# Splitting the output projection's first weights inside the samples' attention, and turning the result rows inside the last MLP

## The reference

```
def run_trunk(x, pos, nsa_cache, page_table, win_cache, ...):
    for l in range(DEPTH):
        h = rms_norm(x, attn_norm_g[l])
        (q, k_cmp, v_cmp, k_slc, v_slc, k_win, v_win, gate_pre, hq, hf, hi, hg) = split_proj(h @ w_in[l])
        ...
        past = nsa_cache[l, page_table]            # samples: 8 pages of 128 rows each
        wk = concatenate([win_cache[l][:, :, 0], k_win])
        ...
        o_nsa = nsa_attention(...)                 # compressed, selected and window branches, with gates
        o_hg, s_fin = hgrn2(...)
        x = x + concatenate([o_nsa, o_hg]) @ w_out[l]
        h2 = rms_norm(x, mlp_norm_g[l])
        x = x + square(relu(h2 @ w_up[l])) @ w_down[l]
    return x, ...
```

## Time and profile before

| | |
|---|---|
| time, median of 3 runs | 2057.99 us (2055.7 to 2062.35) |
| the profiled execution's own time | 2054.93 us |
| its span | 2053.1 us |
| PE busy | 1905.8 us (93%) |
| DVE, ACT, POOL busy | 55%, 40%, 34% |
| mean granted PE clock | 0.966 |

### The profile page before, as it was taken

How to read it: one execution, slowest core, us unless ns; L and a number is a source line. 1 busy time by engine, 2 the same in 40 slices (tenths; PEclk the granted TensorE clock), 3 DMA queues, 4 the chain that set the end, 5 groups by cost and what they waited for, 6 DMA issues and landing times. The chain is left out here.

```text
span 2053.1 us, 38910 instructions
## 1 busy us (share of the span) xinstructions
PE 1905.8 (93%) x15789; PEld 1785.9 (87%) x15789; DVE 1138.6 (55%) x1899; ACT 828.1 (40%) x1809; POOL 692.3 (34%) x470
## 2 busy tenths in 40 slices
PE   6999798988799999999999997989887999999998
PEld 6999555988599999999999984668875999999998
DVE  4589655454455555555528886555535454545454
ACT  4594355353534131313146923544435341313130
POOL 2325435240043333333323542443201333333331
PEclk8999888999999999999999997999999999999999
DMA  4220520432522222222222223222254222222221
GB/s 155 86 80 23 164 66 9 117 93 70 158 83 83 83 83 84 82 87 83 78 85 84 63 73 104 58 64 67 83 154 111 83 71 93 78 92 81 85 82 48
DMA packets 200638, 175.80 MB, mean 86 GB/s; under 512 B 11356, under 2 KB 198030, under 8 KB 200334
## 3 DMA queue, kind: packets, MB, share of 16 engines
q1 hardware_dynamic: 200354, 173.30, 27.7%
q10 hardware_dynamic: 108, 0.03, 0.0%
HBM read 162.67 MB, written 10.62 MB: 84 GB/s over the span
## 5 line engine op out<-in xcount | busy, mean ns | idle before, releaser
L427 POOL TENSOR_TENSOR WX<-RAW,WX 128x2048 fp32r<-128x2048 f32 (+2 forms) x48 | 222.4, 4634 | 523.0 <-ACT WX L423 523.0
L2391 DVE TENSOR_TENSOR sq<-sq 128x288 f32<-128x288 f32 x128 | 156.9, 1231 | 196.8 <-ACT sq L2360 196.8
L427 POOL TENSOR_TENSOR m_wl<-RAW,m_wh 128x2048 fp32r<-128x2048 f32 x36 | 166.5, 4624 | 285.1 <-ACT m_wh L423 285.1
L439 PE MATMUL bank<-UH,m_wl 128*128 128x288 f32 x640 | 188.7, 295 | 0.0
L438 PE MATMUL bank<-UL,m_wh 128*128 128x288 f32 x640 | 188.7, 295 | 0.0
L437 PE MATMUL bank<-UH,m_wh 128*128 128x288 f32 x640 | 188.6, 295 | 0.0
L439 PE MATMUL bank<-UH,WX 128*128 128x288 f32 x576 | 170.0, 295 | 0.0
L438 PE MATMUL bank<-UL,WX 128*128 128x288 f32 x576 | 169.8, 295 | 0.0
L437 PE MATMUL bank<-UH,WX 128*128 128x288 f32 x576 | 169.6, 295 | 0.0
L2410 DVE TENSOR_TENSOR OT<-bank,rstd 128x288 f32<-128x288 f32 x128 | 58.2, 455 | 183.2 <-PE bank L439 183.2
L2413 DVE TENSOR_TENSOR XT<-XT,OT 128x288 f32<-128x288 f32 x128 | 156.3, 1221 | 4.4
(11 more groups left out here) (386 smaller groups left out, 5829.3 us busy)
## 6 DMA issues: line engine op xcount, KB each, us to landing
RAW<-in_w_up SPq DMA_DIRECT2D x32, 1024.0 KB, 5.4
RAW<-in_w_down SPq DMA_DIRECT2D x32, 1024.0 KB, 5.2
RAW<-in_w_in SPq DMA_DIRECT2D x20, 1024.0 KB, 5.3
R<-in_cache_nsa_kv SPq DMA_DIRECT2D x128, 64.0 KB
HT<-in_cache_nsa_kv SPq DMA_DIRECT2D x128, 64.0 KB, 2.6
RAW<-in_w_in SPq DMA_DIRECT2D x6, 1056.0 KB, 5.4
R<-in_cache_nsa_kv SPq DMA_DIRECT2D x48, 128.0 KB, 2.8
out<-R SPq DMA_DIRECT2D x10, 512.0 KB, 5.0
```

The source lines that it names most:

```text
L427: eng.tensor_tensor(S.granule(S.wl, i, w)[:, chunks], S.granule(S.raw, i, w)[:, chunks], S.granule(S.wh, i, w)[:, chunks].bitcast(F32), AL ...
L439: ins = pe.matmul(out, wl[:, c, cols], ah[:, c, n], start=False, stop=(c == KC - 1))
L2391: dve.tensor_tensor(relu[n % 4], relu[n % 4], relu[n % 4], ALU.mult).then_inc(sem("relu_squared"), 1)
```

## The change

Three things are changed.

1. **The first granule's split goes into the samples' attention.** SP loads the first two granules right behind the last sample's past, without its own wait. ACT makes the high part in its program of pair 2, behind the copies of the probabilities, and POOL makes the whole rest then. The MLP block begins with the copies of `OT`. `WX` must be there during the attention, so the attention's own tiles are smaller.
2. **Seven places for the past are written out** in a table, each of three pieces of 1024 words, so that a place may lie in pieces of several tiles. Sample 4's load starts with the block; samples 5 and 6 wait for `s_valued` (the first product of values on PE), where before only 6 did; sample 7 waits for the first pair's values as before.
3. **The result is turned inside the last MLP.** In the last quarter of `w_down` PE turns the prompt's columns of feature chunk m-1 (4 turns) behind the units of chunk m, ACT copies them into `Y`, and SP stores `Y` in four parts (chunks 0 to 3, 4 and 5, 6, 7). Behind the last unit PE turns the samples' 8 chunks and the prompt's last one. The last block, and the clearing of semaphores ahead of it, are gone.

```diff
@@ samples' attention @@
-                    for b in range(4, NB):
-                        if b == RING - 1:
-                            sp.wait_ge(sem("s_valued"), 1)
-                        if b >= RING:
-                            sp.wait_ge(sem("b_valued"), (b - RING) // 2 + 1)
-                        load_past(sp, b)
-                    sp.wait_ge(sem("b_valued"), 2)
+                    load_past(sp, 4)
+                    sp.wait_ge(sem("s_valued"), 1)
+                    load_past(sp, 5)
+                    load_past(sp, 6)
+                    sp.wait_ge(sem("b_valued"), 1)
+                    load_past(sp, 7)
                     for g in range(2):
                         load_out_granule(...)
+                @block.gpsimd
+                def _(pool):
+                    pool.wait_ge(sem("out_hi"), 1)
+                    pool.tensor_tensor(w0_part(1), W0, w0_part(0).bitcast(F32), ALU.subtract)
...
                             act.activation(dst, src, ACT.Copy).then_inc(sem("pT_kept"), 1)
+                        if a == 2:
+                            act.wait_ge(sem("m_w_raw0"), 16 * 3)
+                            act.activation(w0_part(0), W0, ACT.Copy).then_inc(sem("out_hi"), 1)
@@ MLP, PE @@
-                    pe.wait_ge(sem("m_first_lo"), 1)
-                    first_products(pe, bank[2:6], S7, 0, GW, "mix_lo", lambda c: c + 1, "m_w_lo", (UH, UL))
+                    def turn_prompt(c):
+                        pe.wait_ge(sem("m_grown"), 16 * 3 + 2 * c + 2)
+                        if c >= 2:
+                            pe.wait_ge(sem("y_kept"), c - 1)
+                        for t in range(NT):
+                            ins = pe.transpose(bank[c % 2][:, t * P:(t + 1) * P], XT[:, c, t * P:(t + 1) * P], ident)
+                        ins.then_inc(sem("y_turned"), 1)
...
+                    first_products(pe, bank[2:6], S7, 0, GW, "mix_lo", lambda c: c + 1, (UH, UL))
...
+                        if last and kind == "down" and q == 3 and s == 1 and m >= 1:
+                            turn_prompt(m - 1)
+                    if last:
+                        pe.wait_ge(sem("m_added"), RANK[-5])
+                        for c in range(KC - 1):
+                            turn_samples(c)
+                        turn_prompt(KC - 1)
+                        turn_samples(KC - 1).then_inc(sem("ys_turned"), 1)
@@ MLP, ACT @@
-                    split_hi(act, S7, 0, GW, 0)
+                    def keep_prompt(c):
+                        act.wait_ge(sem("y_turned"), c + 1)
+                        act.activation(Y[:, :, c * P:(c + 1) * P], bank[c % 2]..., ACT.Copy).then_inc(sem("y_kept"), 1)
@@ MLP, DVE @@
-                    split_lo(dve, S7, 0, GW, slice(0, KC // 2), "first_lo")
...
+                    if last:
+                        dve.wait_ge(sem("ys_turned"), 1)
+                        for i in range(2):
+                            ins = dve.tensor_copy(YS[:, i * 512:(i + 1) * 512], bank[2 + (len(U7) + i) % 6][0:NS, :])
+                        ins.then_inc(sem("ys_kept"), 1)
@@ MLP, SP @@
+                    if last:
+                        for a, b in ((0, 4), (4, 6), (6, 7), (7, 8)):
+                            sp.wait_ge(sem("y_kept"), b)
+                            sp.dma_start(y_prompt[0, :, a * P:b * P]..., Y[:, :, a * P:b * P]).then_inc(sem("y_stored"), 16)
+                        sp.wait_ge(sem("ys_kept"), 1)
+                        sp.dma_start(y_sample..., YS).then_inc(sem("y_stored"), 16)
```

More of the change, by code:

```diff
@@ L444, in keep_warm, with first_products @@
             pe.matmul(out[:, 0:n], ident, cst[:, 0:n], start=True, stop=True)
-        def first_products(pe, banks, S, i, w, done, counts, second_half=None, operand=None):
+        def first_products(pe, banks, S, i, w, done, counts, operand=None):
             wh, wl = S.granule(S.wh, i, w), S.granule(S.wl, i, w)
@@ L2042, in layer @@
             cmp_scope.close()
+            open_wx()
             smp_scope = ExitStack()
[L2044 to L2048, removed]
+            R2 = smp_scope.enter_context(nc.sbuf_tensor(f"R2s_{l}", [P, SLOT + 14 * P], F32))
+            KTS = smp_scope.enter_context(nc.sbuf_tensor(f"KTS_{l}", [P, 3072], F32, side="right"))
+            slots += [((R2, 0), (R2, 1024), (R2, 2048)), ((R1, 0), (R1, 1024), (R1, 2048)),
+                      ((HT_, 3072), (R2, 3072 + 14 * P), (R1, R_HI))]
+            assert len(slots) == max(PLACE) + 1
             kTb = [KTS[:, i * 1536:(i + 1) * 1536] for i in range(2)]
@@ L2138, in values @@
                         pe.wait_ge(sem("pT_kept"), 4 * a + 4)
-                        for i, (js, past, new) in enumerate(((range(8), past_of, 12), (range(8, 12), window_of, 13))):
+                        for i, (js, new) in enumerate(((range(8), 12), (range(8, 12), 13))):
                             for j in (*js, new):
@@ L2301, in _ @@
                 def _(pool):
-                    for i in range(len(G7)):
-                        split_lo(pool, S7, i, GW, slice(0 if i else KC // 2, KC))
+                    for i in range(1, len(G7)):
+                        split_lo(pool, S7, i, GW)
                     if l + 1 < DEPTH:
@@ L2364, in _ @@
                                 relu_hi(act, n)
+                        if last and kind == "down" and q == 3 and s == 1 and m >= 1:
+                            keep_prompt(m - 1)
                         if u % 4 == 3 and i + 2 < len(G7):
                             split_hi(act, S7, i + 2, GW, u + 1)
+                    if last:
+                        keep_prompt(KC - 1)
                     if l + 1 < DEPTH:
@@ L2417, in layer @@
                 wx[-1][0].close()
[L2418 removed]
+            else:
+                clear_semaphores()
         for l in range(DEPTH):
             layer(l)
[L2424 to L2453 removed]
```

102 lines of the change are left out of this document (41 added, 61 removed).

## The result

| | before | changed |
|---|---|---|
| time, median | 2057.99 us (2055.7 to 2062.35) | 2045.16 us (2044.31 to 2050.49) |
| span of the profiled execution | 2053.1 us | 2042.6 us |
| PE busy | 1905.8 us | 1903.5 us |
| mean granted PE clock | 0.966 | 0.970 |

The ratio of the times is 0.9943 with a 95% interval of 0.9923 to 0.9962, that is 11.7 us less (7.8 to 15.8). The forecast was 2046.0, with 2042 to 2051.5 as its range. Time, range and sign were right; of the sum's three terms the one for the clock was not.

The account below looks back on a forecast made before the run. Only PE's idle stretches, at MLP starts and the end, could be won. Savings of 7.2, 1.5 (clock) and 3.3 took 12.0 from 2054.9, giving 2042.9; the median's 3.1 offset made 2046.0 us, range 2042 to 2051.5.

Parts of the forecast that it names:

- The attention's end: End of the samples' attention: ACT's added round makes it 0.9 us later per layer, bounds nothing to 1.9.
- The first product: Start of each layer's MLP: PE's first product starts 3.6 us earlier, 7.2 for both layers.
- The clock: PE's clock at both MLP starts: four chances in ten each to keep 2.4 GHz, one keeping it likeliest, 1.5 us gained.
- The rival that the clock holds at both starts: Both MLP starts: PE keeps 2.4 GHz after the shorter gap, 1.5 us less, 2044.5; chance 0.13.
- The end: Last MLP and program's end: turning the result between products gives 3.3 us less, bounds 0.9 to 4.5.
- The sum: Whole kernel: 7.2 + 1.5 + 3.3 = 12.0 us less, bounds 6.1 to 16.5.
- the 3.1 that I carried over: Whole kernel: the runs' median stood 3.1 us above the profiled execution, assumed to hold after the change.
- The hold of POOL over pair 3's step: Samples' attention: POOL's work may delay DVE's step on `HT`; about 2 us were left, so costed at nothing.
- the slower rival: Last quarter of the last MLP: PE stands at turns waiting for late additions, 16 us lost, 2062; chance 0.03.
- the one in which nothing moves: Samples' attention: weights land late, so the MLP start's wait only changes its place, 2058; chance 0.04.
- The 7: Samples' attention: the early-issued weights land some 7 us before ACT needs them at 552.2.

Follow-up runs that it names:

- Experiment 3: The changed kernel with ACT's round of the first granule ahead of pair 2's copies of the probabilities, not behind them; 2047.25 us, 0.9942 to the kernel before.
- experiment 5: The kernel before with the first granule's rest made wholly by DVE, POOL only clearing one column of a scratch tile; 2056.34 us in one run.
- experiment 4: The changed kernel with PE multiplying unread constants behind the attention's last turns and ahead of the MLP's first product; 2044.21 us, 0.9932 to the kernel before.
- experiment 1: The changed kernel without the result's turns in the last MLP, the last block and semaphore clearing kept as before; 2052.29 us, 0.9969 to the kernel before.
- experiment 6: The changed kernel with SP again waiting for pair 1's values before it loads the output projection's first granules; 2047.63 us in one run.
- experiment 8: The changed kernel itself run once more, with a second profile; 2049.61 us, 0.9943 to the kernel before.
- experiment 7: The changed kernel with ACT's round ahead of pair 2's copies, PE's products of constants, and samples' rows copied in two steps; 2041.21 us, 0.9908 to the kernel before.

## Why the prediction was right, and where it was not

**The attention's end, 0.9 a layer: right.** Measured 1.0 and 0.9. Experiment 3 takes all but 0.1 of it away by moving ACT's round alone.

**The first product, 3.6 earlier: right.** Measured 3.6 and 3.8. The gap went to the predicted length, 2.69, and `UL` still ends it. Part of the old gap was POOL's hold on the first `UL`: by experiment 5 the second half of the rest cost 1.0 more on POOL than it would have on DVE.

**The clock: the step that failed.** The prediction gave each layer four chances in ten to keep 2.4 GHz, and took 1.5 us from "exactly one of the two". All ten starts with this gap (two layers in the changed kernel and in experiments 1, 3, 6 and 8) fell to 1.2 GHz, nine of them for 3.4 us and one for 6.8. The term was 0. Its price was right: 1.5 a layer, by experiment 4. The rival that the clock holds at both starts came out only where PE was kept at work (experiments 4 and 7).

The chances had been read from gaps elsewhere in the program, one that held and one that fell, as if the length of a gap told the odds. Nearer rows than those of rows 8 would not have corrected it. PE's timeline of the kernel before has the same gap of 2.73 us at the same place of either layer, and its windows show that the clock held after the first and fell after the second:

```profile
231.56 1.17 PE L926 MATMUL bank<-R,HT 32*128 32x128 f32 x32 [2.73 <-DVE R L1112]
...
1240.58 1.33 PE L926 MATMUL bank<-R,HT 32*128 32x128 f32 x22 [2.73 <-DVE R L1112]
```

```profile
232.00:235.00 3.00, 3.00 (x43) 1.23 (x36) 2.37 (x10) 0.00 (x0) 2.77 (x5) 1.00 0.85 239
1241.00:1244.00 3.00, 3.00 (x36) 1.27 (x29) 1.77 (x8) 0.00 (x0) 2.77 (x6) 0.50 0.85 239
```

Over all ten profiles the clock fell at this gap of 2.73 in 17 cases of 20. A gap of 2.1 at 448.2 held in the changed kernel's first profile (1.00 from 449 to 451) and fell in experiment 8's (0.50), with the same program. So the length alone does not decide. Experiment 4 shows that work in the gap keeps the clock; what besides the gap brings it down, and whether a start with this gap could ever hold, stays open.

The Trainium skill, in "TensorE: Matmul & The Clock Gate", "What's actually happening", ties the fall to a whole idle window. By it a short gap would be safe. The runs speak against that: in the first layers of experiments 1 and 3 the fall came 1.2 and 1.1 us after full-speed products had resumed. Ahead of the gap, though, PE had only four short turns between idle stretches of 0.80 and 2.69 us, so the gap was not the only idleness near the fall.

**The end, 3.3: the mechanism right, the size low.** It is 4.0: 6.8 at the end less 2.8 in the stretch with the six groups, of which they are 2.6. They were costed at 3.0. From the last scaling to the end I had 7.0, and it was 6.4: DVE's copies were done 3.1 behind the scaling (2036.16 to 2039.24) and not 3.4, and the 0.3 set aside for a samples' store held up by chunk 7's were not needed, since the latter landed in 2.3.

**The sum.** For an execution like the profiled one the forecast was 12.0 less; the spans differ by 10.5. That is 12.0, less 1.5 for the clock, with 0.7 for the end and 0.2 for the two starts, less the 0.7 and 0.2 of other places. The forecast of the median came closer (2046.0 against 2045.16) for a reason that I can't claim: the profiled execution took 2044.4, 1.5 more than forecast for it, but its distance to the median is 0.8 and not the 3.1 that I carried over. Executions of these kernels lie several microseconds apart (experiment 8), and one of them says little about where the median stands. That the median came within 0.9 of the forecast is luck: the same kernel's second set has 2049.61.

**The rest.** The hold of POOL over pair 3's step occurred (2.45 instead of 0.16) and was covered by 2.21 of idleness. The Trainium skill, in "SBUF — State Buffer", "Who interferes with whom", says that it is a lock held for a whole instruction. This row agrees. POOL's 5.74 in experiment 5 shows it from the other side, and more: POOL's 1.1 of delay are longer than one `UL`, so it stood through the rest of two. PE did not idle at the turns, so the slower rival had no ground, and the weights were early by some 7 us, so the one in which nothing moves had none either. The 7 itself does not follow from its terms: an issue at 536.5 and 4.2 to land would leave 11.5 us until 552.2. The first granule's third transfer, of 512 KB, was issued at 537.89 and landed 8.4 later, at 546.3, and ACT's round began at 553.06, which does leave 6.8.

## What to carry to other kernels

A shorter wait at the start of a block need not bring back the clock, and did not here: look at what PE does in the gap, and where the granted clock falls at its end, fill it with products of constants that end just ahead of the data (1.5 us each here, at no delay). When work is moved from a border between blocks into a block, read on its engine's timeline which instruction stands right behind, and put it ahead of one that waits anyway; that was worth another 0.8 a layer in the trace. Turns that stood in a block of their own cost 0.43 a group between products, and the end after the last scaling went from 13.3 to 6.4 us.

## What the runs showed of the hardware that was not expected

- A gap of 2.69 us on PE went with a fall of the granted clock from 1.00 to 0.50 in ten starts of ten, twice only more than 1 us after work had resumed (in experiment 1 at 568.09, and 0.63 only from 569 to 570), and once within the gap and for 6.8 us instead of 3.4. The same gap of 2.1 at 448.2 held in one execution of the changed kernel and fell in another.
- The hold between POOL and DVE goes both ways: POOL's subtraction took 5.74 instead of 4.62 when it began under DVE's instructions on two SBUF tiles, and a DVE step on 128 by 2 elements stood for 2.45.
- Stores of 256 KB in runs of 512 bytes from 128 partitions landed in 2.3 us, the samples' store from 64 partitions in runs of 4 KB in 2.9.
- Four turns between products of split weights cost 0.43 us, less than the 0.47 that four of a long row of 24 take.
